# The output projection of a two-layer decoder step, from one fp32 product to three fp32r products

## The reference

```python
def project(x, pos, norm_g_l, w_in_l, q_norm_g_l, k_norm_g_l):
    h = rms_norm(x, norm_g_l)
    z = jnp.einsum('btd,dn->btn', h, w_in_l)
    q, k, v, ga, qi, wi, ki, ub, gb, cv, cg, gc = split_columns(z)
...
# each layer
#   A: sparse attention, 8 heads of 64, keys picked by an indexer's top 256
#   B: causal pooling over windows of 2, 4, 8 and 16 tokens, a linear map
#   C: gated depthwise convolution of width 31, layer norm, swish
#   y = concat(A * silu(ga), B * silu(gb), C * silu(gc))   # 1024 wide
#   x = x + y @ w_out                                      # w_out is 1024 x 1024
```

## Time and profile before

| what | value |
|---|---|
| time, median of 3 runs | 844.39 us (842.32 to 845.61) |
| the profiled execution | 840.52 us, span 839.2 us |
| TensorE busy | 751.8 us, 90% |
| VectorE busy | 597.2 us, 71% |
| ScalarE busy | 327.5 us, 39% |
| GpSimd busy | 331.3 us, 39% |
| mean granted TensorE clock | 0.941 |

### The profile page before, as it was taken

One profiled execution on the slowest core, in us unless ns is written; L12 is line 12 of the kernel. 1 busy time (PEld: TensorE's weight loads), 2 busy tenths in 40 slices (PEclk: granted clock), 3 DMA queues, 4 the chain that ended last, 5 costly groups with the idle time before them and its releaser, 6 DMA issues. The chain is left out here.

```text
span 839.2 us, 12922 instructions
## 1 busy us (share of the span) xinstructions
PE 751.8 (90%) x4476; PEld 601.9 (72%) x4476; DVE 597.2 (71%) x1346; ACT 327.5 (39%) x830; POOL 331.3 (39%) x320
## 2 busy tenths in 40 slices
PE   4898869989888898999998889788988898899998
PEld 4895545668777786777998756365877786777888
DVE  3548897999896996434534889989999799632222
ACT  3725345425735332224132443353464633222202
POOL 0033987933744640011110658787255466000000
PEclk8999999999897999999999999899989898999999
DMA  5533040304141555014025304003423156400312
GB/s 173 158 107 104 4 137 14 100 26 131 53 119 44 150 173 201 2 51 139 4 84 139 105 0 120 35 3 102 138 69 69 50 154 211 147 4 1 101 52 103
DMA packets 57282, 75.08 MB, mean 89 GB/s; under 512 B 13233, under 2 KB 32889, under 8 KB 57185
## 3 DMA queue, kind: packets, MB, share of 16 engines
q1 hardware_dynamic: 57106, 74.18, 28.8%
q10 hardware_dynamic: 111, 0.08, 0.0%
HBM read 67.27 MB, written 7.61 MB: 89 GB/s over the span
## 5 line engine op out<-in xcount | busy, mean ns | idle before, releaser
L1181 PE MATMUL R<-x_hi,W_r 128*128 128x268 f32 x448 | 141.0, 315 | 17.5 <-DVE yT L1717 6.4
L1165 PE MATMUL R<-W_r,x_hi 128*128 128x512 f32 (+3 forms) x320 | 127.7, 399 | 18.0 <-DVE W_r L1508 18.0
L1183 PE MATMUL R<-x_hi,W_r 128*128 128x268 f32 x448 | 135.8, 303 | 0.0
L1182 PE MATMUL R<-x_lo,W_r 128*128 128x268 f32 x448 | 135.5, 302 | 0.0
L1194 PE MATMUL R<-yT,W 128*128 128x268 f32 (+2 forms) x768 | 126.4, 322 | 2.9 <-DVE yT L1508 2.9
L1166 PE MATMUL R<-W_r,x_hi 128*128 128x512 f32 (+3 forms) x320 | 123.6, 386 | 0.0
L1194 PEld LDWEIGHTS R<-yT,W 128*128 128x128 f32 x768 | 108.8, 193 | 19.8 <-issue 6.7
L1167 PE MATMUL R<-W_r,x_lo 128*128 128x512 f32 (+3 forms) x320 | 122.9, 384 | 0.0
L1181 PEld LDWEIGHTS R<-x_hi,W_r 128*128 128x128 f32 x448 | 92.1, 206 | 29.2 <-DVE yT L1717 9.5
L1508 DVE SCALAR_TENSOR_TENSOR cc<-uext,params,cc 128x528 f32<-128x528 f32 x120 | 105.8, 928 | 0.0
L779 POOL TENSOR_TENSOR W_r<-W,W_r 128x1024 fp32r<-128x1024 f32 x28 | 66.9, 2402 | 95.6 <-ACT W_r L897 95.5
(11 more groups left out here) (240 smaller groups left out, 1364.9 us busy)
## 6 DMA issues: line engine op xcount, KB each, us to landing
W<-in_w_in SPq DMA_DIRECT2D x52, 512.0 KB, 4.9
KV<-in_cache_k SPq DMA_DIRECT2D x32, 256.0 KB, 2.8
W<-in_w_out SPq DMA_DIRECT2D x8, 1024.0 KB, 7.5
KV<-in_cache_v SPq DMA_DIRECT2D x32, 256.0 KB, 3.7
ubx<-qkv_rows SPq DMA_DIRECT2D x16, 256.0 KB, 3.5
zi<-z_rows SPq DMA_DIRECT2D x16, 196.0 KB, 3.6
W<-in_w_in SPq DMA_DIRECT2D x8, 296.0 KB, 3.3
out_new_k_prompt<-kz SPq DMA_DIRECT2D x8, 256.0 KB, 2.1
```

The lines of the kernel that those rows point to most:

```text
L1165: pe.matmul(out, x_hi[:, kc, rows], hi, start=(kc == 0), stop=False)
L1181: pe.matmul(out, hi[:, cols], x_hi[:, kc, toks], start=(kc == 0), stop=False)
L1182: pe.matmul(out, hi[:, cols], x_lo[:, kc, toks], start=False, stop=False)
L1183: m = pe.matmul(out, lo[:, cols], x_hi[:, kc, toks], start=False, stop=(kc == KC - 1))
```

## The change

The output projection becomes three fp32r products, as in the input projection: `W_hi y_hi`, `W_hi y_lo`, `W_lo y_hi`. A unit is 24 matmuls of 128x268 (L1255 to L1257 of the changed kernel), and there are two halves of tokens instead of three parts: `("out", m, 0)` for m of 0 to 4 at steps 33, 35, 37, 39 and 42, the other eleven after the loop.

- **W_out** comes as 8 loads of 128 output columns (loads 30 to 37) through the ring; ACT copies the high parts of loads 30 to 35 in its iterations 28, 29, 32, 33, 35 and 36 (`HIGH_AT`, step: load) and those of 36 and 37 after the loop; the rest is subtracted on POOL for loads 30 to 35, on DVE for 36 and 37.
- **x** is no longer kept split until it is added: POOL sums `x_end = x_hi + x_lo` for each half (`x_sum`, one instruction over 128x8x268), so that `x_hi` can take y's high part. ACT writes that (`y_high`), DVE the remainder (`y_rest`, into the new tile `yT_r`), both in the iterations 31, 33 and 38 or 39, and after the loop.
- **DVE** takes an output unit with one addition to `x_end` (L1808). The new x is split at the layer's end, by ACT (`new_x_high`) and DVE (`new_x_rest`) in chunks.
- **ga** units: (m,0) at steps 20, 22, 23, 24, (m,1) at steps 26, 28, 29, 31. Step 27 has no unit.
- The first two weight chunks of the next layer are loaded and split after the loop. y's transposes at the end of layer 1 are in another order.

```diff
+GA_STEPS = (26, 28, 29, 31)
+OUT_STEPS = (33, 35, 37, 39, 42)
...
-OUT_PART = [(0, HALF), (HALF, START[4]), (START[4], TOK)]
+OUT_PART = [(0, HALF), (HALF, TOK)]
+LAST_OUT = ([("out", m, 0) for m in range(len(OUT_STEPS), 6)] + [("out", m, 1) for m in range(6)]
+            + [("out", m, x) for x in (2, 3) for m in (6, 7)])
...
+HIGH_AT = {1: 22, 2: 23, 3: 24, 4: 25, 7: 26, 8: 27, 13: 28, 14: 29, 28: 30, 29: 31, 32: 32, 33: 33, 35: 34, 36: 35}
+Y_HALVES = [(4, 8, 0, HALF), (0, 4, 0, HALF), (4, 8, HALF, TOK), (0, 4, HALF, START[4]), (0, 4, START[4], TOK)]
...
+            def x_sum(h):
+
+                wait_unit(pool, ("ga", 3, h))
+                part = (slice(None), slice(None), slice(N_SAMPLE + HALF * h, N_SAMPLE + HALF * h + HALF))
+                xs_s.did(pool.tensor_tensor(x_end[part], x_hi[part].bitcast(F32), x_lo[part].bitcast(F32), ALU.add))
...
+            x_sum(0)
+            rest(30)
+            rest(31)
+            x_sum(1)
+            for m in range(32, 36):
+                rest(m)
...
             def unit_out(u):
+                pe.wait_ge(*yl_s.at(Y_PARTS[h]))
+                wait_split(pe, l, x)
                 for kc in range(KC):
-                    m = pe.matmul(R[:, k, 0:hi - lo], W[:, slot(x), kc % 4, 128 * (u[1] % 4):128 * (u[1] % 4) + 128],
-                                  yT[:, kc, lo:hi], start=(kc == 0), stop=(kc == KC - 1))
+                    w_hi, w_lo, out = w_high(l, x, W_r)[:, kc, :], w_raw(l, x, W_r)[:, kc, :], R[:, k, 0:HALF]
+                    pe.matmul(out, w_hi, x_hi[:, kc, part], start=(kc == 0), stop=False)
+                    pe.matmul(out, w_hi, yT_r[:, kc, lo:hi], start=False, stop=False)
+                    m = pe.matmul(out, w_lo, x_hi[:, kc, part], start=False, stop=(kc == KC - 1))
                 unit_s.did(m)
...
+            def y_rest(n):
+
+                a0, a1, lo, hi = Y_HALVES[n]
+                dve.wait_ge(*yh_s.at(n + 1))
+                yl_s.did(dve.tensor_tensor(yT_r[:, a0:a1, lo:hi], yT[:, a0:a1, lo:hi],
+                                           x_hi[:, a0:a1, N_SAMPLE + lo:N_SAMPLE + hi].bitcast(F32), ALU.subtract))
...
-            for m in range(KC):
-                take(("out", m, 2))
+                if n == 31:
+                    y_rest(0)
+                    y_rest(1)
+                if n == 33:
+                    y_rest(2)
+                if n == 39:
+                    y_rest(3)
+            y_rest(4)
+            for u in LAST_OUT:
+                take(u)
+                if u in (("out", 2, 1), ("out", 3, 1)):
+                    rest(34 + u[1])
```

More of the change, by code:

```diff
@@ L99, in plan @@
     assert len(free) >= len(fill)
+    for n, m in zip(GA_STEPS, range(4)):
+        steps[n].append(("ga", m, 1))
     steps[30] += [("pool", m, h) for m in range(2) for h in range(2)]
-    for n, m in zip((31, 32, 33, 34, 35, 36, 37, 38), range(KC)):
+    for n, m in zip(OUT_STEPS, range(KC)):
         steps[n].append(("out", m, 0))
-    for n, m in zip((39, 40, 41, 42, 43, 43, 44, 44), range(KC)):
-        steps[n].append(("out", m, 1))
     for i in range(NT):
@@ L117 @@
          + [(n, i, 0) for n in ("k", "q", "v") for i in range(NT)])
-UNITS = EARLY + [u for step in PLAN for u in step] + [("out", m, 2) for m in range(KC)]
+UNITS = EARLY + [u for step in PLAN for u in step] + LAST_OUT
 NUM = {u: n for n, u in enumerate(UNITS)}
@@ L246, in program @@
         x_end = sb("x_end", 128, KC, XT)
+        with nc.sbuf_tensor("yT_r", [128, KC, XT], F32R) as yT_r:
+            pass
         yT = sb("yT", 128, KC, XT)
@@ L619, in w_first @@
             def w_first():
-                for m in range(AHEAD, 6):
-                    if l and m < 4:
-                        sp.wait_ge(*unit_s.at(NUM["out", 3, 2] + 1 - len(UNITS)))
-                    elif l:
-                        sp.wait_ge(*unit_s.at(0))
+                for m in range(AHEAD, W_SLOTS):
                     w_load(m)
@@ L1077, in scalar_layer @@
                     PTk_s.did(copy(pT[:, m % 2, 0:i * MAXR], A[:, m % 2, 0:i * MAXR]))
-                if n == SX["ahead"] and l + 1 < DEPTH:
-                    act.wait_ge(*next_w.at(16 * AHEAD))
-                    for m in range(AHEAD):
-                        split_high(act, l + 1, m, next_hi)
                 if n in HIGH_AT:
@@ L1123, in scalar_layer @@
                                      R[:, bank(u), :].rearrange("p (c t) -> p c t", c=4)[:, :, 0:ROWS[i]]))
[L1124 to L1128 removed]
+                if n == 31:
+                    y_high(0)
+                    y_high(1)
+                if n == 33:
+                    y_high(2)
+                if n == 38:
+                    y_high(3)
+            y_high(4)
+            for u in LAST_OUT:
+                square(u)
+                if u in (("out", 2, 1), ("out", 3, 1)):
+                    high(34 + u[1])
+                if u == ("out", 5, 1) and l + 1 < DEPTH:
+                    act.wait_ge(*next_w.at(16 * AHEAD))
+                    for m in range(AHEAD):
+                        split_high(act, l + 1, m, next_hi)
+                if u[1:] in ((7, 2), (7, 3)) and l + 1 < DEPTH:
+                    new_x_high(u[2] - 2)
             if l + 1 == DEPTH:
@@ L1495, in tensor_layer @@
                         unit(u)
-            pe.wait_ge(*y_s.at(3))
-            pe.wait_ge(*ys_s.at(1))
-            for m in range(KC):
-                unit(("out", m, 2))
+            for u in LAST_OUT:
+                unit(u)
                 if l + 1 == DEPTH:
                     for n, (t, g) in enumerate(Y_TURNS):
-                        if Y_AFTER[n] == m:
+                        if Y_AFTER[n] == u:
                             turn_y(n, t, g)
@@ L1915, in vector_layer @@
                     sd(lambda: dve.tensor_scalar(etp, ET8, pn[:, 256:257], None, ALU.mult), "etp")
-                if n == SX["ahead"] + 1 and l + 1 < DEPTH:
-                    dve.wait_ge(*next_hi.at(4 * AHEAD))
-                    for m in range(AHEAD):
-                        split_rest(dve, l + 1, m, next_lo)
                 if n in PV_KEEP:
```

228 lines of the change are left out of this document (120 added, 108 removed).

## The result

The changed kernel takes 863.35 us, the median of four runs (859.73 to 867.77); the kernel before takes 844.81 beside it. The ratio is 1.0241, 95% interval 1.0199 to 1.0282. The forecast was 854, with a range of 834 to 860: the direction was right, the size too small by half. The profiled execution took 859.73 us, the fastest of the four, with a span of 858.4 us against 839.2.

What follows compares the result with a forecast made beforehand. TensorE's work and waits were taken as the bound. Cheaper products, new waits and clock falls summed to +5.3 us in layer 0 and +4.1 in layer 1, +9.4 together: 849.9 profiled, 853.8 median, given as 854; range 834 to 860.

Steps and rivals of the forecast that it cites:

- What bounds the kernel: Whole kernel: TensorE is busy 90% of the span, so only its own work and its waits count.
- the products: Output projection on TensorE: two units of 3.08 us replace 7.48 us per column block, -10.5 us a layer, -21.0 in all.
- POOL and DVE block each other: Late loop steps: a VectorE operation with two SBUF inputs waits for the POOL instruction it meets; a sum takes 4.85 us.
- Up to step 31: Steps before 30: the first POOL sum delays VectorE's `kz<-kz` by 3.7 us; +1.0 us in layer 0, -0.4 in layer 1.
- Step 30: A gate meets a POOL subtraction, so TensorE's 2.1 us wait before the third pooling unit grows by 1.7 us.
- Steps 31 to the end: Before clock costs: steps 31 and 32 -0.5 us a layer; step 33 to the layer's end -2.6 and -0.9 us.
- the border: Between the layers: a new 1.0 us wait, as the new x is split in chunks behind the last unit.
- the wait at step 35: A new 2.2 us wait: the unit needs POOL's `rest(33)` and `y_rest(2)` behind it, with scores 35 queued behind.
- The clock: Behind waits over 2 us before dense work: mostly 1.5 us more each; +5.7 us in layer 0, +4.2 in layer 1.
- Rival (2): No change: the waits come but the clock does not fall at them; -0.5 us, 844 us; chance 0.17.
- Rival (1): Faster: POOL does not hold VectorE up; about 825 us, or partly so 834 to 839; chances 0.15 and 0.08.
- Rival (3): Much slower: the last W_out columns load late, behind cache pages on SP's queue; 857 us and more; chance 0.07.

Runs made afterwards that it cites:

- the filled run: The changed kernel with 12 and 10 useless fp32 products at the ends of TensorE's steps 32 and 34; 858.57 us, ratio 1.0174 to the kernel before.

## Why the prediction was wrong

**What bounds the kernel; the products.** Right. A unit among the loop's steps takes 3.08 us (372.36 to 375.44), as forecast, and one behind another 24 x 0.123 = 2.96 us in the tail, so the products save about 12 us a layer (10.5 forecast). The Trainium skill ("TensorE: Matmul & The Clock Gate", Back-to-back issue gap) has 114 ns for an isolated product of 268 columns, from which 2.74 us a unit is an estimate; the trace after does not agree, with 0.123 us for a product.

**POOL and DVE block each other.** Right: forecast 3.7 us for `kz<-kz`, measured 3.70; forecast 4.85 for a sum, measured 4.71 and 4.73. It is too narrow in one point: operations on a single tensor were held as well (0.28 us became 1.01, 0.35 became 1.90). The Trainium skill ("SBUF — State Buffer", Who interferes with whom) has the shared pair of ports as an exclusive lock; the run with the sums in pieces agrees (0.47 us against 3.70) and shows the hold going by instruction.

**Up to step 31: the step that failed.** "VectorE was hardly ahead, so I follow both lists to step 30: +1.0 us in layer 0 and -0.4 in layer 1." Measured +5.6 and +4.0: 4.6 and 4.4 more than forecast, 9.0 of the 9.8 us by which the forecast of the two spans' difference (9.4, measured 19.2) was short. I had the late operation right and followed it to scores 28, but passed over two things. TensorE waits in step 27 twice, 2.56 us at the transposes of the very values that `kz<-kz` makes, then 2.06 us at the first weighted values: step 28 starts 2.6 us later, where my numbers gave 1.6 (the pass at 311.8 takes 0.57, and scores 28 started at 310.7 before). And the clock: step 28, with 5.4 us of work, ran at 0.60 and took 8.44 us (8.18 in layer 1). The paragraph on the clock lists where layer 0 gets waits of over 2 us and leaves out step 27, though by its own numbers TensorE stood there for 4.7 us, the unit's 3.08 and those 1.6. In layer 0 the runs without the first sum and with the unit in step 27 put 8.0 of the 8.7 us lost here on the sum, and 5.6 of them on its meeting an empty step; in layer 1 it is 6.5 of 7.1, and 2.6.

**Step 30.** Mechanism and sign right, mis-sized: one gate was to be held (+1.7), both were (2.43 and 2.36 us), and the wait grew by 2.6 us.

**Steps 31 to the end.** The sums are right within 1 us: the wait before scores 33 3.24 us (3.75 forecast), at step 35 2.45 (2.2), at the border 0.36 (1.0), at step 44 0.81 (0.9). At two of them this is partly luck. I had put the wait at step 35 on POOL's `rest(33)`; `y_rest(2)` was held by it for 0.66 us (1.93 instead of 1.27), but before that it waited 3.93 us for ACT's `y_high(2)`, and with that copy earlier the whole wait was gone. And before scores 33 the forecast's chain began with the sum; without the sum 1.6 us stayed, behind ACT's `y_high`. The forecast priced ACT's other copies at nothing and had no term for `y_high`.

**The clock.** The rule from the rows held (a wait of over 2 us costs itself and more), and its price was mostly too low: 2.3 us behind scores 33 and 1.5 behind scores 35 by the filled run, 3.0 in step 28, against 1.4 to 1.6. For step 28 no run filled the wait; without the wait it ran at full clock. The clock also fell behind 1.6 us, in the run without the sums, where the rows had it stay full behind 1.5. Rival (2), that it would not fall, is out. Rival (1), POOL not holding VectorE, too. Rival (3), late columns of W_out, never came: TensorE doesn't wait for a weight of W_out anywhere. That the range ended at 860 goes back to the failed step: with its 9.0 us the forecast is 863.

What stays open: why a given spell of half clock comes in one execution and not in the next (step 31 in five of the kernels, step 44 in most), and with it some 3 us in either direction for a single profile.

## What to carry to other kernels

When work goes to GpSimd, list VectorE's operations beside it, those with two SBUF inputs first but also those on one tensor and a scalar (1.90 us for 0.35 here), and price each at the remaining length of the GpSimd instruction, not at its own. Not all are held: VectorE's 17 takes of 128x268 out of PSUM that met GpSimd in the changed kernel, and its passes over the scores, kept their length. The same work on VectorE in its idle time cost less, and in step 27 short instructions did. When a filler is moved, look at what it stood in front of. And put every new wait of TensorE through the clock before adding up: here, in layer 0, 8.6 us (3.0 + 1.8 + 2.3 + 1.5, in steps 28, 30, 33 and 35) came behind 12.9 us of new waits.

## What had not been expected of the hardware

- Eight POOL additions of 268 elements take 5.97 us, one of 2144 takes 4.71, and steps 26 to 29 were 7.6 and 5.8 us shorter with the eight.
- Two VectorE operations on a single tensor took 1.01 us instead of 0.28 and 1.90 instead of 0.35 beside a POOL subtraction.
- Twelve useless products in a wait of 3.2 us saved 2.3 us: the clock stayed at 1.00 over a stretch that had run at 0.68.
- TensorE's clock fell to half (0.55 over 3.3 us) behind 2.8 us of uninterrupted products of 4 and 8 columns, with eight fp32 products of 128 columns (sixteen in the trace) right before and behind them.
